# Index projections multiplied from unnormalised rows, with the tokens' roots applied to the products

## The reference, cut to what matters

```python
def rmsnorm(x, g):
    y = xf * lax.rsqrt(jnp.mean(xf * xf, axis=-1, keepdims=True) + EPS)
    return (y * g.astype(jnp.float32)).astype(x.dtype)

h = rmsnorm(x, norm_mix_g) @ w_in            # then split into q, k, v, iq, iw, ik, su, sv, ga, gb
rel = jax.nn.relu(jnp.einsum('bthd,bsd->bths', iq, ik))
score = jnp.einsum('bths,bth->bts', rel, iw) * IDX_SCALE
_, idx = lax.top_k(score, topk)
...
bias = rel_bias[rel_bucket(q_pos[None, :, None] - idx)]   # added to the attention's logits
```

## Time and profile before

| | us |
|---|---|
| median of 3 runs | 1433.19 |
| lowest, highest | 1429.78, 1434.17 |
| profiled execution, its own time | 1427.83 |
| span of the profile | 1425.2 |
| PE busy | 1348.3 (95%) |
| DVE busy | 802.5 (56%) |
| ACT busy | 417.1 (29%) |
| POOL busy | 332.7 (23%) |

### The profile page before, as it was taken

The page is one execution under the profiler, slowest core; times in us unless marked ns, Lnnn a source line. Parts: engine busy times, 40 slices in busy tenths (PEclk is TensorE's granted clock), DMA queues, the critical chain, the costliest instruction groups (busy, mean ns, idle before and its releaser), DMA issues.

```text
span 1425.2 us, 33293 instructions
## 1 busy us (share of the span) xinstructions
PE 1348.3 (95%) x14298; PEld 1204.3 (85%) x14298; DVE 802.5 (56%) x1174; ACT 417.1 (29%) x591; POOL 332.7 (23%) x427
## 2 busy tenths in 40 slices
PE   7989999988898999889999999999999999999997
PEld 5967789866787876678876799989999999999997
DVE  5377959856497711488811346435666676652222
ACT  4242323346311221111221322223433333322221
POOL 3513322545322100222100013211233222210000
PEclk8899999999999999899999999999999999999998
DMA  6414312331899999999999683244332233242231
GB/s 189 142 49 140 92 60 98 121 126 60 263 395 355 313 362 403 390 374 355 340 354 402 254 305 126 89 138 154 89 89 68 82 89 89 80 128 82 82 90 70
DMA packets 169006, 266.76 MB, mean 187 GB/s; under 512 B 19915, under 2 KB 131964, under 8 KB 159772
## 3 DMA queue, kind: packets, MB, share of 16 engines
q1 hardware_dynamic: 147659, 174.13, 36.2%
q0 software_dynamic: 14320, 78.22, 14.7%
q10 hardware_dynamic: 6880, 12.29, 2.4%
HBM read 240.30 MB, written 24.18 MB: 186 GB/s over the span
## 4 chain that ended last, share of the span: by engine, by line
PE 86%; DMA 4%; DVE 3%; issue 3%; ACT 2%; SPq 1%; POOL 1%; ACTq 0%; DVEq 0%; POOLq 0%
PE PS L1040 17%; PE PS L1042 16%; PE PS L1041 16%; PE PS L1316 5%; PE PS L1348 5%; PE PS L1434 3%; PE PS L1433 3%; PE PS L1432 3%; PE PS L1084 2%; DMA R<-in_cache_v 2%; PE PS L1085 1%; PE PS L1086 1%; DMA R<-in_sg_w_s 1%; PE PS L1217 1%; PE PS L1099 1%
## 5 line engine op out<-in xcount | busy, mean ns | idle before, releaser
L1040 PE MATMUL PS<-xn_hi,WH 128*128 128x288 f32 (+1 forms) x1424 | 435.5, 306 | 6.4 <-DVE xn_lo L1789 3.9
L1041 PE MATMUL PS<-xn_lo,WH 128*128 128x288 f32 (+1 forms) x1424 | 424.2, 298 | 6.5 <-issue 6.5
L1042 PE MATMUL PS<-xn_hi,WL 128*128 128x288 f32 (+1 forms) x1424 | 424.7, 298 | 0.9 <-issue 0.9
L1040 PEld LDWEIGHTS PS<-xn_hi,WH 128*128 128x128 f32 (+1 forms) x1424 | 270.8, 190 | 26.6 <-issue 14.0
L1042 PEld LDWEIGHTS PS<-xn_hi,WL 128*128 128x128 f32 (+1 forms) x1424 | 271.1, 190 | 8.0 <-issue 8.0
L1041 PEld LDWEIGHTS PS<-xn_lo,WH 128*128 128x128 f32 (+1 forms) x1424 | 271.4, 191 | 0.1
L608 DVE TENSOR_TENSOR WL<-W,WH 128x2048 fp32r<-128x2048 f32 (+2 forms) x73 | 154.8, 2120 | 168.8 <-ACT WH L1486 168.7
L1486 ACT ACTIVATE WH<-W 128x2048 fp32r<-128x2048 f32 (+2 forms) x81 | 144.8, 1788 | 110.2 <-PE PS L1434 74.6
L663 POOL DMA_INDIRECT R<-in_cache_k,KROW x64 | 62.5, 977 | 238.7 <-PE PS L1348 93.6
L1528 ACT ACTIVATE STG<-PS 128x576 f32<-128x576 f32 (+2 forms) x44 | 23.3, 529 | 306.0 <-PE PS L1042 196.9
L2025 DVE STREAM_TRANSPOSE R<-R 128x2048 f32<-128x2048 f32 x42 | 96.1, 2298 | 20.9 <-PE PS L1316 12.7
(11 more groups left out here) (312 smaller groups left out, 2395.9 us busy)
## 6 DMA issues: line engine op xcount, KB each, us to landing
R<-in_cache_v SPq DMA_DIRECT2D x128, 512.0 KB, 7.0
W<-in_w_in SPq DMA_DIRECT2D x30, 1024.0 KB
W<-in_w_up SPq DMA_DIRECT2D x44, 512.0 KB
W<-in_w_down SPq DMA_DIRECT2D x16, 704.0 KB
x_scratch<-xT SPq DMA_DIRECT2D x2, 2304.0 KB, 9.8
W<-in_w_branch_a SPq DMA_DIRECT2D x4, 1024.0 KB
W<-in_w_branch_b SPq DMA_DIRECT2D x4, 1024.0 KB
W<-in_w_out SPq DMA_DIRECT2D x4, 1024.0 KB
```

The lines of the kernel that those rows point to most:

```text
L1040: pe.matmul(out, hi[:, k, cols], x.hi_block(n)[:, tokens], start=first, stop=False)
L1041: pe.matmul(out, hi[:, k, cols], x.lo_block(n)[:, tokens], start=False, stop=False)
L1042: return pe.matmul(out, lo[:, k, cols], x.hi_block(n)[:, tokens], start=False, stop=last)
```

## The change: what it does, and the diff

- The index projections `iq` and `ikw` are multiplied from `xg` = rows times gain (ACT rounds the high parts with the gain as scale, DVE makes the low parts in one instruction), without the root. The first tile is written out: all products with the high weights for both halves of the tokens first, those with the low weights after.
- The sums of squares follow the first index tile instead of preceding it. DVE multiplies the roots in while it copies the five tiles out of PSUM (`rooted`); before, ACT copied them.
- `xn1` is still made, since q, k, v and the rest need it, but between the `rooted` copies.
- The six small vector loads go from SP's queue to ACT's, the `vec` transposes ahead of the last x block, and the load of chunk `iq0` ahead of the large load of constants.
- The eight bias products and `iwrep` stand among the `ps` products (`behind_scores`): `iwrep` behind the 4th, bias behind the 7th, 10th, 13th, 16th, 19th, 22nd, 23rd and 24th. `SWM` is made at the end of the prompt's scores.
- On ACT and DVE the first attention query chunk is split before the prompt's scores, the second right behind them (before: the first behind them).
- POOL: bias write and read-back stand behind the index key stores; the 32 `NBr` pieces are spread four behind each step's page loads of s = 4 to 11.

```diff
+    def behind_scores(r, h):
+        n = H * (r - 1) + h
+        if n == 3:
+            return ('iwrep',)
+        return ('bias', n // 3 - 2) if n >= 6 and n % 3 == 0 else ('bias', n - 16) if n > 21 else None
...
 # SP
+            load_chunk(('iq', 0))
             sp.dma_start(CST[:, NKEPT:NCONST], consts[:, NKEPT:NCONST]).then_inc(S_("consts_in"), 16)
-            for i, g in enumerate((norm_mix_g[0], norm_ffn_g[0], norm_final_g)):
...
 # POOL
-            drained(pool, 'bias', H - 1)
-            link(pool.memset(Vn[64:128, :], 0.0))
-            pool.dma_start(bias_scr, BV).then_inc(S_("bias_out"), 16)
...
+            drained(pool, 'bias', H - 1)
+            pool.wait_ge(S_("iqb_ready"), 1)
+            link(pool.memset(Vn[64:128, :], 0.0))
+            pool.dma_start(bias_scr, BV).then_inc(S_("bias_out"), 16)
+            pool.wait_ge(S_("bias_out"), 16)
...
             for s in range(4, 16):
                 filled(pool, 't', s - 4)
                 idx_pages(pool, s, 1)
+                for i in range(4 * s - 16, min(4 * s - 12, 32)):
+                    new_bias_rows(i)
...
 # PE
+            claim(pe, 'iq', 0)
+            pe.wait_ge(S_("high_ready"), 1)
+            for a in range(2):
+                for k in range(KT):
+                    if a == 0:
+                        pe.wait_ge(S_("raw_ready"), k + 1)
+                    pe.matmul(ptile('iq', 0)[:, a, :], first_hi[:, k, :], xg.hi_block(k)[:, s], start=(k == 0), stop=False)
+                    pe.matmul(ptile('iq', 0)[:, a, :], first_hi[:, k, :], xg.lo_block(k)[:, s], start=False, stop=False)
+            pe.wait_ge(*low_count['iq', 0])
...
             for k in range(KT):
                 rms_sum(0, k)
...
-            for m in range(4):
-                project3(('iq', m), split(('iq', m // 2), 256), column(m), xn1,
-                         (lambda k: pe.wait_ge(S_("xn_ready"), k + 1)) if m == 0 else None)
-            project3(('ikw',), split(('ikw',), 72), slice(0, 72), xn1)
+            for m in range(1, 4):
+                project3(('iq', m), split(('iq', m // 2), 256), column(m), xg)
+            project3(('ikw',), split(('ikw',), 72), slice(0, 72), xg)
...
 # ACT
             drained(act, 'x', R - 1, 0)
+            drained(act, 'x', R - 1, 1)
+            drained(act, 'vec')
+            for k in range(KT):
+                if k == 2:
+                    split_high('iq', 0)
+                act.activation(xg.hi_block(k), xT0[:, k, :], ACT.Copy, scale=VT[:, k:k + 1]).then_inc(S_("raw_high"), 1)
             for k in range(4):
                 square(0, None, k)
-            split_high('iq', 0)
+            after('iq', 0)
             root(0)
...
 # DVE
+            def rooted(dst, *tile):
+                filled(dve, *tile)
+                n = dst.shape[0]
+                dve.tensor_tensor(halves(dst), ptile(*tile)[0:n], halves(RS[0])[0:n], ALU.mult).then_inc(drains(*tile), 1)
...
+            for k in range(KT):
+                raw_low(k)
+            split_low(dve, 'iq', 0)
             squares_low()
...
+            after('iq', 0)
+            root_mean(0)
+            for m in range(4):
+                rooted(iqT[:, m, :], 'iq', m)
+                for k in (2 * m, 2 * m + 1):
+                    whole(k)
+                if m == 1:
+                    after('iq', 2)
+            low(xn1, KT - 1, "xn_high", KT, "xn_ready")
+            after('ikw')
+            rooted(IKW[0:72, :], 'ikw')
```

More of the change, by code:

```diff
@@ L1181, in _ @@
             done(last, 'ikwT')
-            pe.wait_ge(S_("iw_ready"), 1)
-            claim(pe, 'iwrep')
-            for p in range(4):
-                last = pe.matmul(bank('iwrep')[:, 8 * p:8 * p + 8], const('selp', TS)[:, P * p:P * p + P],
-                                 IWS[0:TS, 4, :], start=True, stop=True)
-            done(last, 'iwrep')
             drained(pe, 'ikd0')
@@ L1572, in _ @@
                     k += 1
+                    extra = behind_scores(r, h)
+                    if extra and extra[0] == 'bias':
+                        filled(act, *extra)
+                        act.activation(BV[:, extra[1], :], bank(*extra)[:, 0:BIASW], ACT.Copy)\
+                            .then_inc(drains(*extra), 1)
             for s in range(18):
```

156 lines of the change are left out of this document (90 added, 66 removed).

## The result

| | before | changed |
|---|---|---|
| median of 11 runs, us | 1429.78 | 1437.37 |
| lowest, highest | 1425.41, 1436.36 | 1430.64, 1446.45 |
| profiled execution, its own time | 1427.83 | 1430.64 |
| span of the profile | 1425.2 | 1429.0 |

The ratio is 1.005, 95% interval 1.0027 to 1.0073: the change makes the kernel slower, by 3.9 to 10.4 us. The forecast was 1430, with 0.15 for slower; it counted from 1433.2, the median of three runs of the kernel before, where eleven give 1429.8. The profiled execution of the changed kernel is its fastest run, so its trace shows the change at its mildest.

What follows compares the result with a forecast made beforehand. PE carries 86% of the chain; its own gain would be 8.3 us, but POOL's page loads up to step 11 pass on 4.1 or 2.1, taken as 3.1: 1433.2 - 3.1 = 1430.1, said 1430; range 1423 to 1436.

Steps and rivals of the forecast that it cites:

- step 11's transpose: PE's transpose for step 11 of the sample's index: at 152 to 155 against 157.01, 3.1 us earlier, the whole gain.
- The opening: PE up to the rearranging products: first index matmul at 16.7 against 34.13, rearranging products at 64.6 against 74.01, 9.4 earlier.
- The scores: PE's score products with bias products among them: from 67.1, last bias copy at 92.9, sample's transposes 3.8 us earlier.
- The columns' price: PE's float32 products in the scores: 1.85 ns per column, 22.7 us for 12288 columns.
- its 1.7 for the low clock: Start of the scores on PE: 1.7 us added for running at half clock behind small waits.
- The collisions: POOL's page loads with x store and weight chunk in flight: about 2 us lost before; gain 4.1 or 2.1, middle 3.1.
- rival C: Half clock behind the last page wait costs 1.6 us, hand-overs in the opening 1.5 more: 1433 us; chance 18%.
- The rule on waits between groups of products: PE between and behind POOL's page waits: repeated transfer waits each pay the low clock, absorbed except behind the last (case C).
- B: POOL's queue before step 11 doesn't bind and PE's own 8.3 us come through: 1425 us; chance 22%.
- D: Bias products hold the clock down in half the scores, copy at 104.3: 1441 us; decides against from copy 96.0; chance 12%.

Runs made afterwards that it cites:

- The first two experiments: Changed kernel with POOL's whole bias block behind its page loads: 1426.27 us, ratio 0.9983; with only the 32 pieces behind them: 1426.08 us, 0.9983.
- the trace with unread products: Changed kernel plus six 128-row products that nobody reads, three in each of PE's two waits ahead of the scores: 1431.7 us, ratio 0.9997.
- three last variants: Changed kernel with six unread products: 1431.7 us; with the x store behind s = 15's page loads: 1433.01; with weight chunk k0 ahead of s = 14's: 1436.15.

## Why the prediction was wrong

The change came out slower, not faster. Against the kernel before, the forecast was 3.1 us below and the medians are 7.6 above: 10.7 apart, of which the traces account for 6.6 up to step 11. The forecast's mechanism was right, in its order of steps and in its place: the last bias copy starts POOL's chain, the bias block with its wait goes ahead of the pages, four pieces make each step 6.4 long, PE waits 5.7 us in sum (forecast 4 to 6) for page loads of POOL, and the result is what step 11's transpose shows. The first two experiments show that the pieces turn PE's lead into waits. What failed are the sizes, and one term that the sum lacked, the late page of step 9. The forecast had step 11 at 153.9; it came at 160.5. The 6.6 between, by the rows:

| term | forecast | first trace | adds |
|---|---|---|---|
| first of the scores | 67.1 | 69.0 | 1.9 |
| from there to the last bias copy | 25.8 | 27.1 | 1.3 |
| lost in POOL's issues at 117 to 124 | 1.0 | 2.9 | 1.9 |
| five steps of pages and pieces | 6.57 each | 6.41 each | -0.8 |
| last page of step 9, issue to use | 2.0 | 5.0 | 3.0 |
| step 9 to step 11 | 13.1 (POOL) | 12.6 (PE) | -0.5 |

They add up to 6.8; 0.2 is lost in rounding and in the bias block. Each in turn:

*The opening.* Forecast: PE's first index product at 16.7, the first tile's end 27.5, the rearranging products 64.6. Measured 17.78, 29.90, 66.38. The rows were ready at 14.39, where ACT begins to round them, and not at 13.5:

```profile
14.39 1.44 ACT L1601 ACTIVATE xg_hi<-xT,VT 128x576 fp32r<-128x576 f32 x2 [0.38 <-DVE xT L1882]
15.82 1.91 ACT L1528 ACTIVATE WH<-W 128x2048 fp32r<-128x2048 f32 x1
```

The sample's rows needed 9.8 us from issue to landing, before 8.5:

```profile
R<-in_x_sample SPq DMA_DIRECT2D x1, 256.0 KB, 9.8
```

So another queue for the vectors did not keep the rows' landing where it was. The rule of the Trainium skill that the prediction weighed ("DMA: Bandwidth & Descriptors", section "Issuing engines are not separate DMA queues") fits: the vectors' loads run on the same DMA engines as the rows. But chunk `iq0` now stands right behind the rows too, and no run separates the two. The rest of the opening's 1.9 is the first half of the first tile (6.2 from start to start in place of 5.5) and the second (3.8 in place of 3.2), less the sums of squares (7.6 from 29.90 to 37.45, in place of 8.2).

*The scores.* At full clock they are longer than forecast: in the trace with unread products, where the clock is 1.00 throughout, 25.4 us from the first of them (70.52) to the last copy (95.95), where the forecast's terms without its 1.7 for the low clock make 24.1. The columns' price was too low where the kinds alternate: two copies of bias tiles, one pair of products apart:

```profile
93.69 0.49 ACT L1624 ACTIVATE R<-PS 128x384 f32<-128x384 f32 x1 [0.24 <-PE PS L1232]
...
95.58 0.49 ACT L1624 ACTIVATE R<-PS 128x384 f32<-128x384 f32 x1 [0.24 <-PE PS L1232]
```

that is 1.89 for 512 + 384 columns, 2.11 ns each and not 1.85. The low clock adds to this, and its length differs between executions. From the first of the scores to the last bias copy, and the time that the stretches at a low clock cost (length times what the clock lacks of 1):

| trace | us | lost to the clock |
|---|---|---|
| with unread products | 25.4 | 0 |
| changed, first | 27.1 | 1.6 |
| changed, again | 29.6 | 4.3 |
| x store later | 29.6 | 4.3 |
| weight chunk later | 31.6 | 6.3 |

The difference to 25.4 is the loss, within 0.2. The forecast's 1.7 is right for the fastest run only. That is a likely reason why the median is 7.6 us above that of before while the profiled execution is 2.8 above: argued from four traces of the same scores at a low clock, and from the lower median with the unread products, not measured run by run. The kernel before has low stretches in its scores as well, and executions also differ by several us behind the index (1231.4 to 1237.6 in the traces of the changed kernel and its three last variants), so how much of the difference in medians this explains stays open.

*The collisions.* The prediction took half of the 2 us that the trace of before showed; it was 2.9, and the store of x is the cause (shown). The late page of step 9 was in no term. SP's chunk waits for a buffer that PE frees with the last product of the query tile ahead of step 8 (SP's waits from 130 to 150: what it waited for, us, times, longest):

```profile
SPq L715 <- PE PS L1062: 3.9, 1, 3.9
```

and POOL, now late, issues its last page of step 9 into that load. Before, the pages of that step were long in. The cause is shown, too.

*Behind the last wait.* PE went from step 9 to step 11 in 12.6, where the earlier trace rows gave 11.3 for two steps: 1.3 for the low clock, which lasted to 151. That was rival C's price (1.6), and for this trace it holds; in the second trace of the changed kernel the clock stayed low to 155 and the same way took 14.0, 2.7 more. The rule on waits between groups of products, which the prediction took from the Trainium skill ("TensorE: Matmul & The Clock Gate", section "HAM oscillation — how this bites in real kernels"), agrees with these two traces. It doesn't hold each time: with the bias products moved alone, the clock stayed at 1.00 behind a wait of 3.57, and PE went from step 9 to step 11 in 11.3.

*The rivals.* B (POOL doesn't bind, 8.3 us won) was wrong in its size as well: with POOL freed the end of index is only 2.8 to 3.3 earlier. The first transposes were to start at 92.4; there they started at 98.0 and 96.9, with the clock low for longer. C was right as an addition, not as a case: its 1.6 behind the last wait came as 1.3, its 1.5 in the opening as 1.9, on top of the queue. D, the slower one, had the right consequence and the wrong cause: it set the point from which the bias copy decides against the change at 96.0, and the copy came at 96.1 in the fastest trace and at 96.9 to 100.9 in the others. But the clock falls ahead of the first bias product (that stands behind the seventh score product; the clock is already 0.68 at 68 to 70) and comes back among them, and with the bias products moved alone it stayed at 1.00 through all of the scores. It falls around the two small waits before the scores, and stays up when products of all rows fill them. D's 12% was too small, since there were only 3.1 us between the forecast copy and D's point, and the terms ahead of the copy rested on one execution each.

*What each part is worth*, by the end of index against before: raw rows with the earlier split -3.4, the earlier split alone -2.4, bias products among the scores with POOL's new order +8.5, all together +3.9. Each is one trace, and the two traces of the changed kernel lie 1.8 apart (195.2 and 197.1), so the 1.0 between the first two, all that the raw rows would bring of themselves, is not shown.

## What to carry to other kernels

Work that is moved out of another engine's shadow is paid in full where it lands: the eight bias products cost 1.0 us in all under the wait for the roots and 1.0 each among the scores, plus a wait on the queue behind the last of them. When a DMA queue shares out short transfers between loads that someone waits for, compare its time per pair of steps with the consumer's (here 13 against 11 us): if it is longer, any delay at its head is handed on in full, and if it is shorter, it is absorbed (0.6 of 5 us). A forecast with such a chain should give each term ahead of its start an error, for there is no slack to hide them.

## What the runs showed of the hardware

- With 32-row products in PE's two waits the granted clock was 0.54 to 0.50 at 66 to 72, though PE was busy 2.00 of 2.00 us; with 128-row products there, alone or beside the 32-row ones, it was 1.00.
- The granted clock after a wait differs between executions: 0.50 at 148 to 150 at the end of a wait of 3.50, 1.00 throughout behind one of 3.57 in another kernel; one and the same kernel had 1.6 and 4.3 us of its scores lost to it in two traces.
- DMA issues by POOL slow down while a 2.3 MB store is in flight, gaps of 1.2 to 1.8 us in place of 0.6; a 1 MB weight chunk alone left one gap of 0.93.
- A 32 KB page that was issued 0.7 us behind a 1 MB chunk was usable after 5.0 us in place of 2.0.
- Six small DMA issues on ACT took 0.29 to 0.59 us each, over before PE's first transposes (5.66).
